# Multi-head latent attention on one core: stacked rotary query parts, tiles taken in two halves, value tiles copied by ScalarE

## The reference, cut to what matters

```python
q = (rms_norm(cq, q_norm_g) @ w_q_up).reshape(b, s, 16, 192)      # 128 plain + 64 rotary
kv = (rms_norm(ckv, kv_norm_g) @ w_kv_up).reshape(b, s, 16, 256)
k_nope, v = kv[..., :128], kv[..., 128:]
k = concatenate([k_nope, broadcast(k_pe)], -1)                    # rotary part shared by the heads
q, k = rms_norm(q, q_gain), rms_norm(k, k_gain)
q, k = rotate the last 64 of each by position
sc = q @ k.T / sqrt(192)          # masked: a token sees its own and earlier chunks of 64
o = softmax(sc) @ v
return x + (o * silu(gate)) @ w_out
```

## Time and profile before

| | |
|---|---|
| median of 3 runs | 3508.46 us |
| the profiled execution | 3510.67 us, span 3508.9 us |
| PE busy | 3373.1 us, 96% of the span |
| POOL busy | 2095.8 us, 60% |
| DVE busy | 1541.3 us, 44% |
| ACT busy | 695.9 us, 20% |
| mean granted PE clock | 0.98 of full |

### The profile page before, as it was taken

One profiled execution on the slowest core, in us unless ns is written; L12 is line 12 of the kernel. 1 busy time (PEld: TensorE's weight loads), 2 busy tenths in 40 slices (PEclk: granted clock), 3 DMA queues, 4 the chain that ended last, 5 costly groups with the idle time before them and its releaser, 6 DMA issues.

```text
span 3508.9 us, 63813 instructions
## 1 busy us (share of the span) xinstructions
PE 3373.1 (96%) x21506; PEld 2659.4 (76%) x21506; DVE 1541.3 (44%) x3118; ACT 695.9 (20%) x1260; POOL 2095.8 (60%) x3492
## 2 busy tenths in 40 slices
PE   8999999998999989899989998999999999999899
PEld 6777777776888877678867776787878888888677
DVE  3444444445575754571146666314332343323410
ACT  2111111102323220130023343202111121111210
POOL 6444444445676748688753333587676666666566
PEclk9999999999999989899999999999999999999999
DMA  4111111112222213223311111232222222222232
GB/s 149 50 49 43 50 44 49 50 43 62 72 75 68 78 48 90 75 78 93 93 51 40 35 36 42 61 93 84 79 78 72 78 71 78 78 73 77 66 102 78
DMA packets 459579, 239.42 MB, mean 68 GB/s; under 512 B 27901, under 2 KB 456120, under 8 KB 458936
## 3 DMA queue, kind: packets, MB, share of 16 engines
q1 hardware_dynamic: 455656, 232.19, 22.7%
q10 hardware_dynamic: 3792, 5.28, 0.4%
HBM read 233.22 MB, written 4.19 MB: 68 GB/s over the span
## 4 chain that ended last, share of the span: by engine, by line
PE 87%; DVE 6%; issue 3%; POOL 2%; ACT 1%; SPq 1%; DMA 0%; DVEq 0%; ACTq 0%; POOLq 0%; PEldq 0%
PE proj L321 23%; PE proj L322 21%; PE proj L323 21%; PE work L2281 2%; PE work L1927 2%; POOL w_lo L311 2%; PE work L321 1%; PE work L1117 1%; PE work L323 1%; PE work L322 1%; PE work L658 1%; PE work L672 1%; PE work L666 1%; PE work L1920 1%; PE work L640 1%
## 5 line engine op out<-in xcount | busy, mean ns | idle before, releaser
L307 POOL TENSOR_SCALAR w_hi<-raw_weights 128x256 fp32r<-128x256 f32 x1744 | 754.1, 459 | 1397.2 <-PE proj L323 1381.6
L311 POOL TENSOR_TENSOR w_lo<-raw_weights,w_hi 128x256 fp32r<-128x256 f32 x1744 | 1357.3, 808 | 0.0
L321 PE MATMUL proj<-x_hi,w_hi 128*128 128x512 f32 x2976 | 1243.4, 418 | 40.6 <-POOL w_lo L311 12.7
L323 PE MATMUL proj<-x_hi,w_lo 128*128 128x512 f32 x2976 | 1183.4, 398 | 0.0
L322 PE MATMUL proj<-x_lo,w_hi 128*128 128x512 f32 x2976 | 1182.9, 397 | 0.0
L321 PEld LDWEIGHTS proj<-x_hi,w_hi 128*128 128x128 f32 x2976 | 563.6, 189 | 204.8 <-issue 45.3
L323 PEld LDWEIGHTS proj<-x_hi,w_lo 128*128 128x128 f32 x2976 | 562.9, 189 | 137.9
L322 PEld LDWEIGHTS proj<-x_lo,w_hi 128*128 128x128 f32 x2976 | 565.5, 190 | 110.9 <-issue 0.5
L321 PE MATMUL proj<-o_hi,w_hi 128*128 128x512 f32 x256 | 103.5, 404 | 7.2 <-POOL w_lo L311 3.5
L321 PE MATMUL proj<-lat_hi,w_hi 128*128 128x512 f32 x224 | 99.5, 444 | 7.6 <-DVE lat_lo L1736 4.0
L322 PE MATMUL proj<-o_lo,w_hi 128*128 128x512 f32 x256 | 101.9, 398 | 0.0
(11 more groups left out here) (462 smaller groups left out, 4282.9 us busy)
## 6 DMA issues: line engine op xcount, KB each, us to landing
raw_weights<-w_in SPq DMA_DIRECT2D x260, 256.0 KB, 3.1
raw_weights<-b_w_in SPq DMA_DIRECT2D x256, 256.0 KB, 3.1
raw_weights<-a_w_in SPq DMA_DIRECT2D x100, 256.0 KB, 3.2
raw_weights<-w_out SPq DMA_DIRECT2D x64, 256.0 KB, 3.0
raw_weights<-a_w_out SPq DMA_DIRECT2D x64, 256.0 KB, 3.0
raw_weights<-b_w_out SPq DMA_DIRECT2D x64, 256.0 KB, 3.0
raw_weights<-a_w_kv_up SPq DMA_DIRECT2D x32, 256.0 KB, 2.8
mix<-x SPq DMA_DIRECT2D x4, 1024.0 KB, 8.0
```

Of the source, the lines that this page charges most:

```text
L307: pool.tensor_scalar(part(hi_v, s % 2, q), part(raw_v, s, q), 1.0, 1.0, ALU.mult, ALU.mult).then_inc(hi_done, 1)
L311: pool.tensor_tensor(part(lo_v, s % 2, q), part(raw_v, s, q), part(hi_v, s % 2, q).bitcast(F32), ALU.subtract).then_inc(w_split, 1)
L321: pe.matmul(out, w_h, a_h, start=start, stop=False)
L323: return pe.matmul(out, w_l, a_h, start=False, stop=stop)
```

## The change

1. **Five score matmuls.** The rotary query of a head gets a tile of its own with its high part in the head's 64 rows and its low part in the other 64 (`q_rope[h]`). The high part of the rotary keys, `kr_hi[h]`, now fills all 128 rows (the same 64 rows twice), so that one matmul gives high by high and low by high. A second multiplies by `kr_lo[h]`, zero in the other head's rows. S has three plain and two rotary matmuls. ACT and DVE make the two halves apart (`hqr0`, `hqr1`, `lqr0`, `lqr1`), and the key's rotary steps go over 128 rows.
2. **Order before S of block 0.** On DVE the low part of head 1's query (`lq1`) and of its rotary part (`lqr1`) move into turns 0 and 2 of the pipe.
3. **Value tiles** 5 and 6 are taken by ACT (`take_values`) in place of DVE.
4. **The next pair's tiles** 0 and 1 are taken by DVE in turn 8, tiles 2 and 3 in turn 9; before all four were taken in turn 9.
5. **Fillers.** 6 groups before S of block 0 (4 before), 2 in turns 1 and 2 (1 before), the rest of the turns as they were: 20 groups in the pipe in place of 16. The 4 groups at the head of `mla_scale_pe` are gone. The rotation's matmul now writes work[1] in place of work[3].

```diff
-        MA_ACT = steps("mla_act", "sq2 sq0 sq1 sq3 sq4 rows hq0 hq1 hqr vt0 vt1 hk0 hkr0 hk1 hkr1 " + piped("e{0}", "pT{0}", ""))
-        MA_DVE = steps("mla_dve", "qc qs qrr ms msk " + RSQRT + " lq0 lq1 lqr k0 kr0 lk0 lkr0 k1 kr1 " +
+        MA_ACT = steps("mla_act", "sq2 sq0 sq1 sq3 sq4 rows hq0 hqr0 hqr1 hq1 vt0 vt1 hk0 hkr0 hk1 hkr1 " + piped("e{0}", "pT{0}", ""))
+        MA_DVE = steps("mla_dve", "qc qs qrr ms msk " + RSQRT + " lq0 k0 kr0 lqr0 lk0 lkr0 k1 kr1 " +
                        piped("sc{0} nb{0}", "rec{0} p{0}", "g{0}", (1, 0, 2))
-                       .replace("nb1", "nb1 lk1").replace("nb2", "nb2 lkr1"))
+                       .replace("nb0", "nb0 lq1").replace("nb1", "nb1 lk1").replace("nb2", "nb2 lqr1 lkr1"))
...
-            run(part, 4)
+            run(part, 8)
             mla_scale_pe(pe, 0, part)
-            pe.wait_ge(kr_zeroed, 4)
+            pe.wait_ge(kr_zeroed, 2)
...
-                run(part, 16 - used)
+                run(part, MLA_AHEAD - used)
...
-            run(part, 4)
+            run(part, 20 - MLA_AHEAD)
+            pe.wait_ge(tile_free, T_MLA + 7 * p + 3)
+            pe.matmul(work[1][:, :], common[:, C_ROT:C_ROT + P], m_qg[:, :], start=True, stop=True)\
+              .then_inc(MA_PE.mark("rot"), 1)
+            run(part, 3)
             pe.wait_ge(MA_DVE.sem, MA_DVE.after(p))
-            pe.wait_ge(tile_free, T_MLA + 7 * p + 3)
-            pe.matmul(work[3][:, :], common[:, C_ROT:C_ROT + P], m_qg[:, :], start=True, stop=True)\
-              .then_inc(MA_PE.mark("rot"), 1)
-            run(part, 2)
-
-            run(part, 1)
...
-            yield 4
+            yield 6
...
-                    multiply(pe, work[k % 2][:, :], qr_hi[:, qs], qr_lo[:, qs], kr_hi[h], kr_lo[h], False, True)\
-                        .then_inc(MA_PE.mark(f"S{k}"), 1)
-                    yield 1
+                    pe.matmul(work[k % 2][:, :], q_rope[h][:, qs], kr_hi[h], start=False, stop=False)
+                    pe.matmul(work[k % 2][:, :], q_rope[h][:, qs], kr_lo[h], start=False, stop=True)\
+                      .then_inc(MA_PE.mark(f"S{k}"), 1)
+                    yield 2 if k in (1, 2) else 1
...
-            for h in range(2):
-                high(q_hi[h], m_q[h][:, :], f"hq{h}")
-            need(MA_DVE, "qrr")
-            high(qr_hi, m_qr[:, :], "hqr")
+            take_values(0)
...
+            high(q_hi[0], m_q[0][:, :], "hq0")
+            need(MA_DVE, "qrr")
             for h in range(2):
+                high(q_rope[h][HEADS[h], :], m_qr[HEADS[h], :], f"hqr{h}")
+            high(q_hi[1], m_q[1][:, :], "hq1")
...
+            def take_values(h):
+                act.wait_ge(tile_free, T_MLA + 7 * p + 5 + h)
+                tile_done(act, U_MLA + 4 * p + UNIT_OF[5 + h])
+                act.activation(m_vr[h][:, :], proj[(5 + h) % 4][:, :], ACT.Copy).then_inc(tile_free, 1)
...
+                if k == 0:
+                    low_q(1)
                 if k == 1:
                     low_k(1)
                 if k == 2:
+                    low_q_rope(1)
                     low_k_rope(1)
-                if k == HB + 1:
+                if k >= HB:
                     chain()
-                    take_next()
+                    take_next((0, 1) if k == HB else (2, 3))
```

More of the change, by code:

```diff
@@ L1781, in build @@
         m_sq, sq_parts = zip(*(take_m(f"sq{n}") for n in range(5)))
-        q_hi, qr_hi, k_hi = sq_parts[0:2], sq_parts[2], sq_parts[3:5]
+        q_hi, k_hi = sq_parts[0:2], sq_parts[3:5]
         m_qg = a8.take("mla_q_rope_gained", SEQ)
-        m_qr, qr_lo = take_m("q_rope")
+        m_qr = a8.take("mla_q_rope", SEQ)
         m_kr = a8.take("mla_k_rope", SEQ)
-        m_tmp = a8.take("mla_tmp", SEQ)
+        m_tmp, tmp_part = take_m("tmp")
+        q_rope = (sq_parts[2], tmp_part)
         kr_hi = [a6.over(f"mla_k_rope_hi{h}", at, SEQ, F32R)[:, :] for h, at in enumerate((r_all_at, lat_sq_at))]
@@ L1834, in mla_project @@
                     yield
+        MLA_AHEAD = 20
         def mla_pe(pe):
@@ L1949, in mla_heads_act @@
             act.activation(m_e[0][:, :], work[2][:, :], ACT.Copy).then_inc(MA_ACT.mark("rows"), 1)
+            def take_values(h):
[3 more added lines that the diff above has]
+            take_values(0)
             high = lambda out, x, name: act.activation(out, x, ACT.Copy).then_inc(MA_ACT.mark(name), 1)
-            need(MA_PE, "sums")
+            high(q_hi[0], m_q[0][:, :], "hq0")
+            need(MA_DVE, "qrr")
             for h in range(2):
-                high(q_hi[h], m_q[h][:, :], f"hq{h}")
-            need(MA_DVE, "qrr")
-            high(qr_hi, m_qr[:, :], "hqr")
+                high(q_rope[h][HEADS[h], :], m_qr[HEADS[h], :], f"hqr{h}")
+            high(q_hi[1], m_q[1][:, :], "hq1")
             for h in range(2):
@@ L1958, in mla_heads_act @@
                 act.activation(m_vt[h][:, :], work[h][:, :], ACT.Copy).then_inc(MA_ACT.mark(f"vt{h}"), 1)
+                if h == 0:
+                    take_values(1)
             for h in range(2):
-                hs = HEADS[h]
                 need(MA_DVE, f"k{h}")
@@ L1963, in mla_heads_act @@
                 need(MA_DVE, f"kr{h}")
-                high(kr_hi[h][hs, :], m_kr[hs, :], f"hkr{h}")
+                high(kr_hi[h], m_kr[:, :], f"hkr{h}")
             for k in pipe:
@@ L1978, in mla_dve @@
         def mla_dve(dve):
-            take_q_and_k(dve, 0)
+            take_q_and_k(dve, 0, range(4))
             for h in range(2):
-                for part in (kr_hi[h], kr_lo[h]):
-                    dve.memset(part[HEADS[1 - h], :].bitcast(F32), 0.0).then_inc(kr_zeroed, 1)
+                dve.memset(kr_lo[h][HEADS[1 - h], :].bitcast(F32), 0.0).then_inc(kr_zeroed, 1)
             with dve.Fori(0, A_HEADS // 2 - 1) as p:
-                mla_heads_dve(dve, p, lambda: take_q_and_k(dve, p + 1))
-            mla_heads_dve(dve, A_HEADS // 2 - 1, lambda: None)
+                mla_heads_dve(dve, p, lambda tiles: take_q_and_k(dve, p + 1, tiles))
+            mla_heads_dve(dve, A_HEADS // 2 - 1, lambda tiles: None)
             stage_end(dve, 6, [(MA_DVE.sem, MA_DVE.after(A_HEADS // 2)), (tile_free, T_MLA + 7 * (A_HEADS // 2))])
         def take_tile(dve, p, j):
+            if j == 0:
+                dve.wait_ge(tile_free, T_MLA + 7 * p)
             if j in (0, 3, 4):
@@ L1992, in take_tile @@
                 tile_done(dve, U_MLA + 4 * p + UNIT_OF[j])
-            dst = (m_q[0], m_q[1], m_qg, m_k[0], m_k[1], m_vr[0], m_vr[1])[j][:, :]
+            dst = (m_q[0], m_q[1], m_qg, m_k[0], m_k[1])[j][:, :]
             if j == 2:
@@ L1999, in take_tile, with take_q_and_k @@
             ins.then_inc(tile_free, 1)
-        def take_q_and_k(dve, p):
-            for j in range(4):
+        def take_q_and_k(dve, p, tiles):
+            for j in tiles:
                 take_tile(dve, p, j)
@@ L2015, in mla_heads_dve @@
             need(MA_PE, "rot")
-            done(dve.tensor_tensor(m_tmp[:, :], work[3][:, :], sin[:, :], ALU.mult), "qs")
+            done(dve.tensor_tensor(m_tmp[:, :], work[1][:, :], sin[:, :], ALU.mult), "qs")
             chain()
             done(dve.tensor_tensor(m_qr[:, :], m_qr[:, :], m_tmp[:, :], ALU.add), "qrr")
-            take_tile(dve, p, 5)
             need(MA_PE, "sums")
@@ L2026, in mla_heads_dve @@
             rsqrt(dve, MA_DVE, p, work[3][:, 0:32], m_small[:, 16:32], m_small[:, 32:48], rs)
-            take_tile(dve, p, 6)
             dve.wait_ge(tile_free, T_MLA + 7 * p + 5)
@@ L2036, in mla_heads_dve @@
                                         f"kr{h}")
+            low_q = lambda h: low(q_lo[h], m_q[h][:, :], q_hi[h], f"q{h}")
+            low_q_rope = lambda h: low(q_rope[h][HEADS[1 - h], :], m_qr[HEADS[h], :], q_rope[h][HEADS[h], :], f"qr{h}")
+            low_q(0)
             for h in range(2):
-                low(q_lo[h], m_q[h][:, :], q_hi[h], f"q{h}")
-            low(qr_lo, m_qr[:, :], qr_hi, "qr")
-            for h in range(2):
-                hs = HEADS[h]
                 need(MA_PE, f"inv{h}")
@@ L2044, in mla_heads_dve @@
                                               ALU.mult, ALU.mult), f"k{h}")
-                done(dve.tensor_tensor(m_kr[hs, :], k_rope[hs, :], work[2 + h][hs, :], ALU.mult), f"kr{h}")
+                if h:
+                    dve.wait_ge(MA_DVE.sem, MA_DVE.done("lkr0", p))
+                done(dve.tensor_tensor(m_kr[:, :], k_rope[:, :], work[2 + h][:, :], ALU.mult), f"kr{h}")
                 if h == 0:
+                    low_q_rope(0)
                     low_k(0)
```

## The result

The changed kernel takes 3487.14 us (median of 4 runs, 3486.18 to 3487.62) against 3508.71 before; the ratio is 0.9936, 95% interval 0.9919 to 0.9953. 3485 was forecast. The profiled execution has a span of 3485.3, 23.6 less than before. Of these, 22.3 lie between the first filler start of the MLA stage (1801.62 before, 1800.74 after) and the first matmul of the output projection (2214.01, now 2190.80).

A forecast was written before the change was run, and what follows sets the result against it. PE was taken as the bound, busy 3373.1 of 3508.9 us. At -3.1 a pair, seven pairs gave -22 and the eighth -1.8: -24 from 3510.67, 3487, median 3485; own range 3481 to 3489, whole range 3472 to 3501.

The forecast's parts named there:

- The bound: PE's stream: eight score matmuls fewer a pair, 0.23 to 0.24 each, -1.86 a pair where PE is the bound.
- Before block 0: PE's wait of 2.4 for the low rotary keys goes, DVE's chain shrinking from 6.75 to 5.35, with a margin of 0.25.
- Turn 8: New PE wait at the start of tile 4 for DVE's copy of tile 0: 2.35 in issue, 2.1 idle.
- Narrow, but it holds: Turns 2 to 7: the chain score, mask, exponential, division keeps slack with five matmuls, 3.8 against 3.9, so nothing waits.
- the cost of nothing for the two low parts: Turns 0 and 2: DVE would stand idle during ACT's exponential (0.81), and added filler gives T another 0.70 each.
- T of block 7: After turn 8's new gap T finds its division done, so its wait of 0.25 goes.
- The sum: A pair -2.4, clock -0.73, together -3.1; seven pairs -22, the eighth -1.8; in all -24.
- The clock: PE's clock falls behind two of the seven new waits, bounds 0 and 7, at 1.27 each; before, six of seven.
- The case in which all seven new waits lower it: Rival: the clock falls at every new wait in turn 8; -17, 3491; chance 0.20.
- A wait before block 0 that stays: Rival: keys come 2.7 later, the old 2.4 stands beside the new 2.1; 3508; chance 0.10.
- the slower case: Rival: waits before block 0 and in turn 8 both stand and each lowers the clock; +1.4 a pair, 3518; chance 0.05.
- No new wait: Rival: the start of tile 4 in turn 8 finds tile 0 taken, no clock falls; -41, 3467; chance 0.07.

The follow-up runs named there:

- x1: Changed kernel with a sixth matmul in each score block again (low part of plain query by low part of plain key): 3503.15 us, ratio 0.998 to before.
- x5: Kernel before with part 1 of the change alone (five score matmuls, stacked query), ACT's order and rotation bank as changed: 3500.73 us, ratio 0.9969.
- x2: Changed kernel with fillers in their old places and all four tiles taken in turn 9: 3480.77 us, ratio 0.9917 to before.
- x8: Changed kernel with all query low parts made before block 0 again (part 2 undone): 3502.25 us, ratio 0.9974 to before.
- x4: Changed kernel with both value tiles copied by DVE again, at their old places: 3491.55 us, ratio 0.9945 to before.
- x3: Changed kernel with tile 0 of the next pair taken by DVE at the end of turn 5: 3468.62 us, ratio 0.9881 to before.
- x10: Changed kernel with 5 filler groups before block 0 in place of 6 and 1 in turn 2 in place of 2: 3476.57 us, ratio 0.9903.
- x6: Changed kernel with the low part of head 1's rotary query made in turn 3 in place of turn 2: 3489.74 us, ratio 0.9938.

## Why the prediction was right, point by point

**The bound.** PE's stream bounds the turns: x1 prices a score matmul at 0.23, forecast 0.23 to 0.24.

**Before block 0.** The wait of 2.4 went, as forecast. The margin is 0.84, forecast 0.25. The chain on DVE was 4.96 for 5.35, although two of its steps were held (below): `lk0` takes 0.78 in place of 1.21. It now starts 0.2 ahead of the subtraction of POOL's split (1918.30), but whether that makes it shorter is not shown, since in x5 it took 0.72 with the subtraction under way. That the margin came out larger is luck. ACT rounded the keys by 1918.32, ahead of need. Fillers and order each hold the wait off: without the fillers 0.46 comes back (x2), without the order 1.34 (x8), without ACT's copies nothing in the seven pairs, with 0.05 to spare (x4).

**Turn 8.** Forecast: no issue from 1954.47 on for 2.35, 2.1 in idle time. Measured 2.27 and 2.02. The estimate of 0.5 for the division alone was right (0.48). That the wait sits where the filler belongs to tile 4, behind the copy, is shown two ways: taking tile 0 earlier (x3) and shifting the groups (x10) each remove it. As a price the gap in issue is the right measure, as x3 shows; taking idle time for both waits did little harm, 2.55 - 2.27 in place of 2.40 - 2.02.

**T of block 2.** The step that was wrong: "Narrow, but it holds", and the cost of nothing for the two low parts moved into turns 0 and 2. Turn 0 bears its one. Turn 2 has two, of which `lqr1` takes 1.19 where it starts beside POOL's split, `lkr1` behind it 0.69: an idle time of 0.53 a pair, a gap of 0.69 in issue, 4.8 in all. x6 and x8 show the two low parts as the cause (with one or both away the wait at T of block 2 is gone), and x6 that it cannot be pushed one turn on. The slack that the five matmuls took away counts too: with six (x1) the gap there is 0.31.

**T of block 7** lost its 0.25, as forecast. Two small waits of the kernel before, which also went, were overlooked. In the timeline of before, behind the start at 2030.68, T of block 0 starts 0.50 after the last filler matmul where a step is 0.23:

```profile
2034.72 0.40 PE L323 MATMUL proj<-lat_hi,w_lo 128*128 128x512 f32 x1
2035.22 0.66 PE L1920 MATMUL work<-common,mla_probs 128*128 128x128 f32 x4
```

The second filler group of turns 1 and 2 covers it and a smaller one a turn later (0.16). These, some 0.4 together (0.3 behind a fall of the clock), offset more than half of the 0.69; x2 has both back.

**The sum.** A pair without falls went from 50.20 to 47.95, -2.25, forecast -2.4. By the gaps in issue it is -1.86 - 2.55 - 0.25 - 0.43 + 2.27 + 0.69 = -2.13, so 0.1 stays unexplained. With falls, 51.18 to 48.23: -2.95, forecast -3.1. The eighth pair: the wait fell by 1.8 (5.39 to 3.59) where 1.4 was forecast, but from there to the output projection 30.59 became 30.82 where some -0.4 was forecast, so -1.6 in place of -1.8. The clock has a part in this. Windows of 3 us from the eighth start on show a granted clock of 0.50, 0.50, 0.50 and 0.92 in the changed kernel (2160 to 2172; the same in its second profile, to within 0.01), and 0.50, 0.87 and 1.00 before (2183.4 to 2192.4). In x4 it is 0.50 and then 0.98, and the same stretch took 30.18.

The time itself was met better than its parts. The stage gave 22.3 of the 24 that were forecast, and the other 1.3 of the profile's 23.6 lie outside it, where a start of the stage may differ by 5 from profile to profile. That the profiled execution took 3487.09 where 3487 was forecast is luck to that extent.

**The clock.** Forecast two falls by 1.27, measured one by 1.62. The 1.27 was the dearest in the trace of before: its five periods with a fall are 51.25 to 51.47 against 50.20, so 1.05 to 1.27, on average 1.17. The count repeats with a kernel: twice 1 of 7 now, 6 and 7 of 7 before. The case in which all seven new waits lower it (3491) did not come, but x1 has it, with the same wait of 2.02 and starts 51.0 apart. That the gap's length decides, which I had as a reason for few falls, is refuted by x1. The Trainium skill's "TensorE: Matmul & The Clock Gate", section "What's actually happening", has the gate on a free-running schedule; the runs agree with it in that one gap length gave 1, 2, 5 and 7 falls.

**The held instruction.** `lqr0` started at 1917.19, 0.04 after the end of the step before, and `lk0` at 1918.10, 0.03 after: both were held, as the rule of the Trainium skill's "VectorE: DVE Perf Modes", section "Two Vector instructions with no wait between them", has it. At 0.1 each it did not matter.

**The rivals.** A wait before block 0 that stays, and the slower case built on it, needed ACT late by 2.7; ACT was early. No new wait: x3 is that case made real, at 3468.6, forecast for it 3467.

Added up, the parts give: part 1 alone -11 (x5); parts 1 to 3 -29 (x2); all five -22.

## What to carry to other kernels

When filler moves, ask what each group belongs to. The group that opens a new tile brings that tile's wait with it: here moving the fillers took waits of 0.46, 0.34 and 0.23 a pair away and put a gap of 2.27 in their place. Price a stall by the gap between two starts, and place the copy that frees a buffer as early as that buffer's last reader allows (x3, 19 below the changed kernel). A move of small steps on a second engine into a turn needs that turn's worst duration, beside what the third engine does then.

## What the runs showed of the hardware

One and the same idle time of PE, 2.02, was followed by the low clock once in seven (the changed kernel, twice over), twice (x4, x6), five times (x8, whose wait before block 0 of 1.34 was followed by none) and seven times (x1). A fall cost 1.05 to 1.27 a pair ahead of score matmuls and 1.62 ahead of filler, T and V. So the length of the gap does not set the count. Small edits changed it: in the profiled executions of x8 and x1, 6 and 10 of what they took over the changed kernel are the clock's. Kernels with a longer period had more falls (47.96 to 48.1 without a fall: one or two; 48.87: five; 51.0 with falls: seven), but falls lengthen the period themselves and no run varied it alone, so the cause stays open. The five runs of x4 lie from 3486.19 to 3493.77, and the fastest has the highest mean granted clock (0.983, the others 0.980 to 0.981): a difference of a few us between two versions of this kernel may be the clock's.
